# A one-core hybrid encoder layer: one weight conversion moved ahead of the mixed sums on ScalarE, and 144 transposes of the identity added on TensorE around three phase borders

## The chip, the cores and the metric

The kernel runs on one core of a Trainium2 chip. The metric is the device time in microseconds of one execution; the kernel before takes 3360.77 us (median of 3 runs, 3360.53 to 3361.61). The engines are TensorE (PE, its weight loads PEld), VectorE (DVE), ScalarE (ACT), GpSimd (POOL) and SyncE (SP), which issues most of the transfers. TensorE's clock has two levels, 2.4 and 1.2 GHz; the profile gives the granted clock as a share of the upper one.

## The reference

One layer over 2048 tokens of width 1024, float32:

```python
xn = rms_norm(h, g_attn_pre);  proj = xn @ w_in                       # 1024 -> 2304
ya = mixer_a(qa, ka, va)   # grouped-query attention, q/k normalised and rotated, softmax over all keys
yb = mixer_b(qb, kb, vb)   # three dilated windows with a relative-position bias, merged
y  = concat(rms_norm(ya, g_out_a), rms_norm(yb, g_out_b)) @ w_out
h  = h + rms_norm(y, g_attn_post)
f  = square(relu(rms_norm(h, g_mlp_pre) @ w_ff1)) @ w_ff2             # 1024 -> 4096 -> 1024
h  = h + rms_norm(f, g_mlp_post)
h  = h + sigmoid(rms_norm(h, g_ple) @ w_ple_gate) * (p @ w_ple_proj)
```

## The kernel before, in words

**Phases.** Four phases stand one behind the other, each a block of five engine programs with a barrier of all engines at its end: `project_phase`, `mixer_a_phase`, `mixer_b_phase`, `feed_phase`. Order inside a phase is written out by hand; engines meet only through semaphores, and each engine works its own list strictly in order.

**Numbers.** A float32 product is made of two parts. A matrix x is split into an upper half (x rounded to the matmul type, by a copy) and a lower half (x minus the upper half); three matmuls per pair of tiles (`PAIRS`) then give the product.

**The feed phase** walks over 4 blocks of 512 tokens. For each it does the MLP in 4 groups g. A group has 22 weight chunks, listed in `FF`: eight chunks f0 to f7 (24 matmuls each) make the hidden layer, then fourteen chunks (12 matmuls each) make the second MLP product in seven block products n = 0 to 6 of a fast 2x2 scheme (BLOCK_OF, GOES_TO), with two chunks q = 0, 1 for each. They are called 0.0, 0.1, 1.0, 1.1, 2.0 and so on here. Products 0 and 1 take plain quarters of the hidden layer. Products 2 to 6 take sums of quarters, the **mixed sums**: for each of four row groups m of the hidden layer VectorE forms five sums (`mix`, L2394 to L2398), ScalarE writes their upper half (`mixed_hi`, L2191), VectorE their lower half (`mixed_lo`, L2387). TensorE waits before chunk 2.0 for the lower half of the last row group, m = 3.

**Weight chunks.** A raw chunk lands in one of four slots of `w_raw` and is split into one of four slots of `w_sp` (which bear the names feed_v_hl twice, feed_qT and feed_kT, since they lie in the memory of those). For f chunks GpSimd makes both halves (L1860, L1863). For the others ScalarE makes the upper half (`weight_hi`, L2186) and GpSimd the lower (`low`, L1863). `weight_hi` of chunk i waits for its transfer and for TensorE to have begun chunk i - 3; TensorE waits for the lower half. `weight_hi(i + 3)` stands at step i of ScalarE's list.

**Gathering.** When a block product is done, VectorE adds it to two areas of `total` (`gathered`, L2413, eight instructions of 128x512 for products 0 and 1; L2410 where it is the first of a block). Chunk 2.0 writes the banks of product 0, so its first half (t = 0) waits for VectorE's second add, and its second half for the fourth. These adds stand behind `mixed_lo(g, 3)` in VectorE's list.

**Borders.** TensorE's last work in a phase is L446/L449 (project), `fold_out` in the mixers. In mixer B it then starts with four transposes of the identity (L1469) into score banks and waits for its first keys; in the feed phase with `turn(0, 0)`, eight transposes of the first normalised rows, and `first_out(0, 0)` (L1991).

Of the kernel before, what the change touches and what calls it, by code (L numbers as in the profile page):

```python
# [20 lines left out]
P = 128  # L21
# [15 lines left out]
BANK = 512  # L37
# [153 lines left out]
def project_phase(nc, x, w_in, g_pre, g_q, g_k, rope, ident_d, rel_bias, onehot, scr, step, ident, first):  # L191
# [21 lines left out]
    with ExitStack() as ctx:  # L213
# [168 lines left out]
        def _(pe):  # L382
# [39 lines left out]
            for it in range(NBLK // 2):  # L422
                for u in range(2):
                    b = it * 2 + u
                    for i in range(NCH):
                        c = NCH * u + i
                        if b == 0 and i == 0:
                            bias_product(b, 0)
                            continue
                        g = GROUP_OF[i]  # L430
                        n_k = 8 if g == 1 else 4
                        width = CH // n_k
                        k0 = 4 if i > 0 and GROUP_OF[i - 1] == g else 0
                        first, last = k0 == 0, k0 + n_k == KD
                        pe.wait_ge(w_lo, it * (2 * NCH) + NRAW + c + 1)
                        w = [h[:, c % NSPL, :].rearrange("p (k n) -> p k n", k=n_k) for h in w_sp]
                        for t in range(TT):
                            if i == 0:
                                pe.wait_ge(lo_done, b * (2 * TT) + 2 * t + 2)
                            if first:  # L440
                                pe.wait_ge(evicted, b * (NG * TT) + TT * g + t + 1)
                            for kk in range(n_k):
                                for q, (a, m) in enumerate(PAIRS):
                                    begin, end = first and kk == 0 and q == 0, last and kk == n_k - 1 and q == 2
                                    if g in DIMS_FIRST:
                                        mm = pe.matmul(acc[t][:], w[a][:, kk, t * P:(t + 1) * P], xT[u][m][:, k0 + kk, :],  # L446
                                                       start=begin, stop=end)
                                    else:
                                        mm = pe.matmul(acc[t][:, 0:width], xT[u][a][:, k0 + kk, t * P:(t + 1) * P],  # L449
                                                       w[m][:, kk, :], start=begin, stop=end)  # L450
                            if last:
                                mm.then_inc(acc_done, 1)
                        if not last:
                            mm.then_inc(w_used, 1)
                        if i % 2 == 1 and b + 1 < NBLK:
                            turn(b + 1, i // 2)
                        if i in BIAS_AT:
                            bias_product(b, BIAS_AT[i])

        @block.scalar  # L460
        def _(act):
# [682 lines left out]
def mixer_b_phase(nc, scr, step, ident, heads, feed, consts):  # L1144
# [13 lines left out]
    with ExitStack() as ctx:  # L1158
# [254 lines left out]
        def _(pe):  # L1413
# [53 lines left out]
            for sc in score:  # L1467
                for at in (BANK, 2 * BANK - P):
                    pe.transpose(sc[:, at:at + P], ident[:], ident[:])  # L1469
            pe.wait_ge(set_done, 2)  # L1470
            pe.wait_ge(pre_lo, len(FIRST_ORDER))
            scores(0, 0, 0)
# [4 lines left out]
            for h in range(NHB):  # L1477
                par = h % 2
                for n in range(NU):
# [11 lines left out]
                    values(N, h, par, n)  # L1491
                    fold_out(N + 1, n - 1)
            fold_out(NHB * NU + 1, NU - 1)

        @block.scalar
        def _(act):
# [139 lines left out]
def feed_phase(nc, x, w_ff2, w_tail, pT_d, scr, out, step, ident, feed):  # L1636
# [45 lines left out]
    with ExitStack() as ctx:  # L1682
# [205 lines left out]
        def _(pe):  # L1888
# [89 lines left out]
            def first_out(t, n):  # L1978
# [15 lines left out]
                                mm.then_inc(w_used, 1)  # L1994
                mm.then_inc(acc_done, 1)

            turn(0, 0)
            for t in range(TT):
                for n in range(2):
                    first_out(t, n)  # L2000
                    at = 2 * t + n
                    if at < 3:
                        turn(1 + at, 1 + at)
                    if at in (4, 6):
                        turn(TT + at // 2 - 2, at // 2 - 2)
# [84 lines left out]
        def _(act):  # L2090
# [89 lines left out]
            def body(b, u, end=False):  # L2180
# [24 lines left out]
                    act.activation(plain(0, half, m), part(m, half, half), ACT.Copy).then_inc(c_hi, 1)  # L2205

                for i, c in enumerate(FF):
                    if i + 3 < NFF and FF[i + 3][0] == "m":
                        weight_hi(i + 3)
                    if c[0] == "f":  # L2210
                        hidden_hi(c[1], c[2])
                        if c[2] % 2 == 0 and c[2] > 0:
                            mixed_hi(c[1], c[2] // 2 - 1)
                    elif c[2:] == (0, 0):
                        mixed_hi(c[1], 3)
                    if i in NORM_Y and not end:
                        t = NORM_Y[i]
                        y_norm(norm_at(b) + t, t, (y_dma, b * 144 + 32 * (t + 1)), y_in)
                    if i in TURN_Y and not end:
                        t = TURN_Y[i]  # L2220
                        turned_hi(turn_at(b) + t, t, 0, xT)
                    if i == p_at(end):
                        act.wait_ge(y_dma, b * 144 + (16 if end else 32 * TT + 16))
                        act.wait_ge(acc_done, acc_at(b) + (2 * NP * (GROUPS - 1) + 2))
                        act.activation(flat(0, 0, 1), y_in[:], ACT.Copy).then_inc(p_hi, 1)
# [423 lines left out]
```

## Time and profile before

| | |
|---|---|
| time, median of 3 runs | 3360.77 us (3360.53 to 3361.61) |
| time of the profiled execution | 3360.36 us |
| its span, first to last instruction | 3358.6 us |
| PE busy | 3294.1 us, 98% of the span |
| DVE, ACT, POOL busy | 68%, 55%, 55% |
| PE L1906 on the chain that ended last | 41% |
| mean granted clock | 0.996 |

Busy shares are means over four phases. What a change is worth is read where an engine waits: the profile names for each idle stretch the instruction that ended it. "L1906" is the line that issues nearly all matmuls of the feed phase. Two instructions of one engine overlap a little in the records (an instruction's record starts while the one before drains), so the spacing of starts is the better measure of a rate.

### The profile page before, as it was taken

How to read it: one execution, taken by the hardware profiler on the slowest of the kernel's cores; microseconds unless marked ns; L12 is line 12 of the kernel's file. 1: busy time of each engine (PE TensorE's matmuls, PEld its weight loads, DVE VectorE, ACT ScalarE, POOL GpSimd, SP SyncE). 2: the span in 40 equal slices, each digit the busy share in tenths (PEclk: the TensorE clock that was granted, in tenths of full speed). 3: DMA queues.
4: the chain of work that ended last, by engine and by line, in shares of the span. 5: the costliest groups of instructions: out<-in, count | busy, mean ns of one | idle time of the engine just before them, and what ended most of it. 6: DMA issues, size and time to landing. Idle time of an engine off the chain costs nothing.

```text
span 3358.6 us, 48304 instructions
## 1 busy us (share of the span) xinstructions
PE 3294.1 (98%) x17246; PEld 2767.0 (82%) x17246; DVE 2278.8 (68%) x4080; ACT 1853.5 (55%) x3576; POOL 1851.7 (55%) x1434
## 2 busy tenths in 40 slices
PE   8999999999999989998999999999999999999999
PEld 7888878888888879997888888888888888888887
DVE  6556579999999989997646565555746556565555
ACT  3221178888888879998434354344543435443333
POOL 5555534454452168883477732777407776057771
PEclk9999999999999999999999999999999999999999
DMA  5554433444442234344244456444474444744444
GB/s 192 165 185 152 142 104 139 154 169 157 157 143 75 62 88 104 95 99 173 78 138 151 151 194 251 144 154 147 163 250 163 147 155 144 262 155 143 143 149 158
DMA packets 223915, 503.39 MB, mean 150 GB/s; under 512 B 105428, under 2 KB 123420, under 8 KB 204476
## 3 DMA queue, kind: packets, MB, share of 16 engines
q1 hardware_dynamic: 214332, 486.57, 43.9%
q10 hardware_dynamic: 9344, 13.73, 1.1%
q8 instruction: 138, 2.26, 0.3%
q14 instruction: 101, 0.83, 0.1%
HBM read 417.09 MB, written 95.58 MB: 153 GB/s over the span
## 4 chain that ended last, share of the span: by engine, by line
PE 44%; DVE 4%; ACT 2%; POOL 2%; issue 1%; DMA 1%; SPq 0%; ACTq 0%; DVEq 0%
PE feed_bank L1906 41%; DVE feed_sums L2397 1%; PE feed_bank L1991 1%; PE feed_bank L1897 1%; POOL feed_v_hl L1863 1%; POOL feed_qT L1863 0%; PE feed_bank L2014 0%; DMA feed_y_in<-scr_yB 0%; DVE feed_xT L2321 0%; ACT feed_rl L2201 0%; ACT feed_rl L2203 0%; PE feed_bank L2046 0%; POOL feed_kT L1863 0%; ACT feed_v_hl L2186 0%; DVE feed_sums L2394 0%
## 5 line engine op out<-in xcount | busy, mean ns | idle before, releaser
L1863 POOL TENSOR_TENSOR feed_v_hl<-feed_w_raw,feed_v_hl 128x1024 fp32r<-128x1024 f32 x176 | 437.6, 2496 | 138.6 <-ACT feed_v_hl L2186 133.0
L1906 PE MATMUL feed_bank<-feed_v_hl,feed_comb 128*128 128x512 f32 x1776 | 416.5, 390 | 3.1 <-POOL feed_v_hl L1863 3.1
L1906 PEld LDWEIGHTS feed_bank<-feed_v_hl,feed_comb 128*128 128x128 f32 x1776 | 331.8, 188 | 74.5 <-POOL feed_v_hl L1863 6.3
L1126 DVE TENSOR_TENSOR mixa_pT<-mixa_turned,mixa_pT 128x512 fp32r<-128x512 f32 x512 | 350.9, 685 | 58.9 <-ACT mixa_pT L1068 52.5
L1068 ACT ACTIVATE mixa_pT<-mixa_turned 128x512 fp32r<-128x512 f32 x512 | 306.7, 599 | 118.7 <-PE mixa_turned L1004 99.6
L949 PE MATMUL mixa_out_acc<-mixa_pT,mixa_v_hl 128*128 128x512 f32 x1028 | 365.7, 437 | 0.2
L2413 DVE TENSOR_TENSOR feed_total<-feed_total,feed_bank 128x512 f32<-128x512 f32 x352 | 223.9, 682 | 190.2 <-PE feed_bank L1906 187.4
L2382 DVE TENSOR_TENSOR feed_comb<-feed_rl,feed_comb 128x256 fp32r<-128x256 f32 x128 | 138.9, 1085 | 312.1 <-ACT feed_comb L2205 311.7
L1906 PE MATMUL feed_bank<-feed_xT,feed_v_hl 128*128 128x512 f32 x1488 | 344.3, 390 | 3.1 <-ACT feed_rl L2201 3.1
L2201 ACT ACTIVATE feed_rl<-feed_bank 128x512 f32<-128x512 f32 x128 | 76.4, 597 | 490.2 <-PE feed_bank L1906 483.5
L1906 PEld LDWEIGHTS feed_bank<-feed_xT,feed_v_hl 128*128 128x128 f32 x1488 | 280.2, 188 | 62.0 <-issue 3.7
L1093 DVE TENSOR_REDUCE mixa_nmax<-mixa_score 128x1 f32<-128x1024 f32 x256 | 312.6, 1221 | 8.1 <-PE mixa_score L936 1.3
L1004 PE MATMUL mixa_turned<-layer_ident,mixa_prob 128*128 128x128 f32 x2048 | 307.2, 273 | 0.9 <-DVE mixa_pT L1126 0.7
L1004 PEld LDWEIGHTS mixa_turned<-layer_ident,mixa_prob 128*128 128x128 f32 x2048 | 251.7, 141 | 59.8 <-DVE mixa_pT L1126 3.7
L1038 ACT ACTIVATE mixa_prob<-mixa_score,mixa_nmax 128x1024 f32<-128x1024 f32 x256 | 286.2, 1118 | 3.7 <-DVE mixa_nmax L1093 3.6
L936 PE MATMUL mixa_score<-mixa_kT,mixa_qT 128*128 128x512 f32 x1024 | 279.5, 394 | 3.6 <-ACT mixa_prob L1038 2.4
L1863 POOL TENSOR_TENSOR feed_qT<-feed_w_raw,feed_qT 128x1024 fp32r<-128x1024 f32 x88 | 221.6, 2518 | 95.8 <-ACT feed_qT L2186 93.1
L1863 POOL TENSOR_TENSOR feed_kT<-feed_w_raw,feed_kT 128x1024 fp32r<-128x1024 f32 x88 | 218.1, 2478 | 38.0 <-ACT feed_kT L2186 35.2
L936 PEld LDWEIGHTS mixa_score<-mixa_kT,mixa_qT 128*128 128x128 f32 x1024 | 191.6, 188 | 50.3 <-ACT mixa_prob L1038 4.2
L1906 PE MATMUL feed_bank<-feed_qT,feed_comb 128*128 128x512 f32 x888 | 213.7, 391 | 2.2 <-POOL feed_qT L1863 2.2
L1906 PE MATMUL feed_bank<-feed_kT,feed_comb 128*128 128x512 f32 x888 | 212.7, 390 | 2.2 <-POOL feed_kT L1863 1.2
L1906 PEld LDWEIGHTS feed_bank<-feed_qT,feed_comb 128*128 128x128 f32 x888 | 165.7, 188 | 39.0 <-POOL feed_qT L1863 4.7
(263 smaller groups left out, 7099.6 us busy)
## 6 DMA issues: line engine op xcount, KB each, us to landing
feed_w_raw<-scr_wT SPq DMA_DIRECT2D x160, 512.0 KB, 3.3
feed_w_raw<-w_tail_dram SPq DMA_DIRECT2D x128, 512.0 KB, 3.5
proj_w_raw<-w_in_dram SPq DMA_DIRECT2D x36, 1024.0 KB, 5.3
feed_v_hl<-scr_wG SPq DMA_DIRECT2D x34, 1024.0 KB, 5.1
feed_w_raw<-w_ff_dram SPq DMA_DIRECT2D x64, 512.0 KB, 3.4
feed_qT<-scr_wG SPq DMA_DIRECT2D x17, 1024.0 KB, 4.8
feed_kT<-scr_wG SPq DMA_DIRECT2D x17, 1024.0 KB, 5.1
scr_table<-scr_bias SPq DMA_DIRECT2D x8, 1520.0 KB, 9.0
```

The source lines that it names most:

```text
L936: mm = pe.matmul(score[:, at * BANK:(at + 1) * BANK], qT[g][:, h, :], kT[g][part][:, kc * BANK:(kc + 1) * BANK], start=part == 0, stop=par ...
L949: mm = pe.matmul(out_acc[half][:], v_hl[:, s, g, :], pT[part][:, s % NR, :], start=s % (NT // 2) == 0 and part == 0, stop=s % (NT // 2) == ...
L1004: mm = pe.transpose(turned[s % 2][:, h * P:(h + 1) * P], prob[w][:, h, s * P:(s + 1) * P], ident[:])
L1038: act.activation(prob[par][:, h, half * 2 * BANK:(half + 1) * 2 * BANK], score[:, 2 * (c % 2) * BANK:2 * (c % 2 + 1) * BANK], ACT.Exp, bia ...
L1068: act.activation(pT[0][:, s % NR, :], turned[s % 2][:], ACT.Copy).then_inc(hi_done, 1)
L1093: ve.tensor_reduce(nmax[:, par, c // G, c % G:c % G + 1], score[:, 2 * (c % 2) * BANK: 2 * (c % 2 + 1) * BANK], AXX, ALU.max, negate=True) ...
L1126: ve.tensor_tensor(pT[1][:, s % NR, :], turned[s % 2][:], pT[0][:, s % NR, :].bitcast(F32), ALU.subtract).then_inc(lo_done, 1)
L1863: pool.tensor_tensor(w_sp[slot][:, 1, :], w_raw[:, slot, :], w_sp[slot][:, 0, :].bitcast(F32), ALU.subtract).then_inc(w_lo, 1)
L1906: mm = pe.matmul(dst, lhs, rhs, start=start, stop=stop)
L2201: act.activation(hidden(m, half), first_bank(b, g, j)[:], ACT.Relu).then_inc(f_relu, 1)
L2382: ve.tensor_tensor(plain(1, half, m), part(m, half, half), plain(0, half, m).bitcast(F32), ALU.subtract).then_inc(c_lo, 1)
L2413: ve.tensor_tensor(at, at, acc[2 * (n % 2) + t][:], ALU.add if sign > 0 else ALU.subtract).then_inc(ev_dve, 1)
```

## The change

In the feed phase, at the step of chunk 0.0 of every group, ScalarE now makes the upper half of chunk 2.0 (`weight_hi(i + 4)`) ahead of the upper half of the last mixed sums; it made it right behind them before, at the step of chunk 0.1, where it is left out now. On TensorE transposes of the identity are added, which nobody reads and which wait for nothing: 24 at the end of the project phase, 36 after the four that mixer B begins with, 28 at the end of mixer B, and in the feed phase 32 ahead of `turn(0, 0)` and 24 behind it.

```diff
--- before.py
+++ after.py
@@ -456,6 +456,8 @@
                         if i in BIAS_AT:
                             bias_product(b, BIAS_AT[i])
+            for _ in range(24):
+                pe.transpose(tp[0][:, 0:P], ident[:], ident[:])
@@ -1467,6 +1469,8 @@
             for sc in score:
                 for at in (BANK, 2 * BANK - P):
                     pe.transpose(sc[:, at:at + P], ident[:], ident[:])
+            for _ in range(36):
+                pe.transpose(score[1][:, BANK:BANK + P], ident[:], ident[:])
@@ -1491,5 +1495,7 @@
             fold_out(NHB * NU + 1, NU - 1)
+            for _ in range(28):
+                pe.transpose(score[0][:, 0:P], ident[:], ident[:])
@@ -1994,7 +2000,14 @@
+            def keep_on(count):
+
+                for _ in range(count):
+                    pe.transpose(acc[3][:, 0:P], ident[:], ident[:])
+
+            keep_on(32)
             turn(0, 0)
+            keep_on(24)
             for t in range(TT):
@@ -2205,13 +2218,14 @@
                 for i, c in enumerate(FF):
-                    if i + 3 < NFF and FF[i + 3][0] == "m":
+                    if i + 3 < NFF and FF[i + 3][0] == "m" and FF[i - 1][2:] != (0, 0):
                         weight_hi(i + 3)
                     if c[0] == "f":
                         hidden_hi(c[1], c[2])
                         if c[2] % 2 == 0 and c[2] > 0:
                             mixed_hi(c[1], c[2] // 2 - 1)
                     elif c[2:] == (0, 0):
+                        weight_hi(i + 4)
                         mixed_hi(c[1], 3)
```

ScalarE's list in the feed phase, block 0, group 1, from the end of f7 on, before. L2201, L2203 and L2205 are the ReLU, the square and the upper half of the plain quarter; L2186 is an upper half of a weight chunk, named by its slot:

```order
 L2201 ACTIVATE feed_rl<-feed_bank 128x512
 L2203 ACTIVATE feed_rl<-feed_rl 128x512
 L2205 ACTIVATE feed_comb<-feed_rl 128x256
 L2186 ACTIVATE feed_v_hl<-feed_w_raw 128x1024
 L2191 ACTIVATE feed_comb<-feed_sums 128x5x256
 L2186 ACTIVATE feed_qT<-feed_w_raw 128x1024
 L2186 ACTIVATE feed_kT<-feed_w_raw 128x1024
```

and the same place after (the lines are numbered 13 higher):

```order
 L2214 ACTIVATE feed_rl<-feed_bank 128x512
 L2216 ACTIVATE feed_rl<-feed_rl 128x512
 L2218 ACTIVATE feed_comb<-feed_rl 128x256
 L2199 ACTIVATE feed_v_hl<-feed_w_raw 128x1024
 L2199 ACTIVATE feed_qT<-feed_w_raw 128x1024
 L2204 ACTIVATE feed_comb<-feed_sums 128x5x256
 L2199 ACTIVATE feed_kT<-feed_w_raw 128x1024
```

The conversion into feed_qT (chunk 2.0) and the mixed sums have changed places; nothing else on ScalarE has moved, and no other engine's list has in the feed phase's blocks. On TensorE this stands at the border of mixer B and the feed phase, before:

```order
 L1465 MATMUL mixb_out_acc<-layer_ident,mixb_o_sum 128x128 x2
 L1158 UNCONDITIONAL_BRANCH
 L1887 UNCONDITIONAL_BRANCH
 L1897 MATMUL feed_bank<-layer_ident,feed_xn 128x128 x8
 L1991 MATMUL feed_bank<-feed_v_hl,feed_xT 128x512 x12
```

and after:

```order
 L1467 MATMUL mixb_out_acc<-layer_ident,mixb_o_sum 128x128 x2
 L1499 MATMUL mixb_score<-layer_ident 128x128 x28
 L1160 UNCONDITIONAL_BRANCH
 L1893 UNCONDITIONAL_BRANCH
 L2006 MATMUL feed_bank<-layer_ident 128x128 x32
 L1903 MATMUL feed_bank<-layer_ident,feed_xn 128x128 x8
 L2006 MATMUL feed_bank<-layer_ident 128x128 x24
 L1997 MATMUL feed_bank<-feed_v_hl,feed_xT 128x512 x12
```

Three runs of transposes are new there (L1499, L2006 twice), and the order of the rest is as it was.

## Rows read from the trace of the kernel before

**Rows 1.** Who TensorE waited for, whole span: us in total, times, longest.

```profile
PE feed_bank L1906 <- POOL feed_v_hl L1863: 3.1, 8, 0.6
PE feed_bank L1906 <- POOL feed_qT L1863: 2.2, 6, 0.4
PE feed_bank L1906 <- POOL feed_kT L1863: 1.2, 2, 0.6
```

**Rows 2.** Timeline, block 0, group 1: start, length, instruction, [idle before].

```profile
1774.32 1.04 ACT L2186 ACTIVATE feed_v_hl<-feed_w_raw 128x1024 fp32r<-128x1024 f32 x1
...
1775.22 2.88 PE L1906 MATMUL feed_bank<-feed_kT,feed_comb 128*128 128x512 f32 x12
1775.44 2.69 POOL L1863 TENSOR_TENSOR feed_v_hl<-feed_w_raw,feed_v_hl 128x1024 fp32r<-128x1024 f32 x1 [1.52 <-ACT feed_v_hl L2186]
...
1775.79 2.62 DVE L2397 TENSOR_TENSOR feed_sums<-feed_rl 128x256 f32<-128x256 f32 x1
...
1778.33 0.41 DVE L2398 TENSOR_TENSOR feed_sums<-feed_rl 128x256 f32<-128x256 f32 x1
1778.78 1.28 ACT L2191 ACTIVATE feed_comb<-feed_sums 128x1280 fp32r<-128x1280 f32 x1 [3.42 <-DVE feed_sums L2398]
1779.96 1.05 ACT L2186 ACTIVATE feed_qT<-feed_w_raw 128x1024 fp32r<-128x1024 f32 x1
1780.09 1.49 DVE L2387 TENSOR_TENSOR feed_comb<-feed_sums,feed_comb 128x1280 fp32r<-128x1280 f32 x1 [1.34 <-ACT feed_comb L2191]
...
1781.09 2.77 POOL L1863 TENSOR_TENSOR feed_qT<-feed_w_raw,feed_qT 128x1024 fp32r<-128x1024 f32 x1 [2.96 <-ACT feed_qT L2186]
1781.49 4.87 DVE L2413 TENSOR_TENSOR feed_total<-feed_total,feed_bank 128x512 f32<-128x512 f32 x8
...
1783.91 3.01 PE L1906 MATMUL feed_bank<-feed_qT,feed_comb 128*128 128x512 f32 x12 [0.37 <-POOL feed_qT L1863]
```

**Rows 3.** Timeline, block 0, group 0: GpSimd and VectorE's sums.

```profile
1666.25 1.23 POOL L1860 TENSOR_SCALAR feed_kT<-feed_w_raw 128x1024 fp32r<-128x1024 f32 x1
1666.49 1.26 DVE L2397 TENSOR_TENSOR feed_sums<-feed_rl 128x256 f32<-128x256 f32 x1
1667.57 2.42 POOL L1863 TENSOR_TENSOR feed_kT<-feed_w_raw,feed_kT 128x1024 fp32r<-128x1024 f32 x1
1667.67 2.59 DVE L2398 TENSOR_TENSOR feed_sums<-feed_rl 128x256 f32<-128x256 f32 x1
```

**Rows 4.** Timeline, block 0, group 3, at chunk 1.0.

```profile
1941.78 1.32 ACT L2191 ACTIVATE feed_comb<-feed_sums 128x1280 fp32r<-128x1280 f32 x1
1942.02 2.42 POOL L1863 TENSOR_TENSOR feed_v_hl<-feed_w_raw,feed_v_hl 128x1024 fp32r<-128x1024 f32 x1 [3.60 <-ACT feed_v_hl L2186]
...
1943.14 2.65 DVE L2387 TENSOR_TENSOR feed_comb<-feed_sums,feed_comb 128x1280 fp32r<-128x1280 f32 x1
...
1944.39 3.66 POOL L1863 TENSOR_TENSOR feed_qT<-feed_w_raw,feed_qT 128x1024 fp32r<-128x1024 f32 x1
```

**Rows 5.** Windows, PE: stretch, length, busy (x), clock, DMA share, GB/s.

```profile
431.83:435.32 3.49, 0.01 (x2) 1.00 0.20 75
1194.62:1204.86 10.24, 6.16 (x17) 0.50 0.48 112
1576.91:1590.54 13.63, 5.08 (x15) 0.50 0.80 316
```

**Rows 6.** Timeline at the start of mixer B.

```profile
1193.88 0.63 PE L1469 MATMUL mixb_score<-layer_ident 128*128 128x128 f32 x4 [1.05 <-PEq L664]
...
1198.70 0.66 PE L1425 MATMUL mixb_score<-feed_kT,feed_qT 128*128 128x384 f32 x1 [4.20 <-DVE mixb_kT L1562]
...
1209.32 0.44 PE L1425 MATMUL mixb_score<-feed_kT,feed_qT 128*128 128x384 f32 x1 [0.89 <-POOL feed_qT L1326]
```

**Rows 7.** The chain that ended last, start of the feed phase: start, length, what.

```profile
1579.07 1.33 ACT feed_junk L2125 x4
...
1582.89 1.13 PE feed_bank L1897 x4
...
1587.43 7.19 PE feed_bank L1991 x24
1594.62 0.87 PE feed_bank L1897 x8
1595.49 5.47 PE feed_bank L1991 x24
```

## The prediction, made before the changed kernel ran

> **What bounds the kernel now.** I read the busy shares first: TensorE is busy 98% of the span, so a change gains only where it fills a gap of TensorE or raises its clock, and it loses wherever it makes TensorE wait. Next the table of who TensorE waited for. In the feed phase it waits 16 times for GpSimd's lower half of a weight chunk (8 + 6 + 2 times), 3.1 + 2.2 + 1.2 = 6.5 us [rows 1]. Looked at group by group, 13 of these waits are alike, 0.37 us each, at chunk 2.0 (all groups but the last one of blocks 0, 1 and 2), and three of 0.6 us lie at a later chunk of those last groups. Then the timeline around one of the 13 [rows 2]. The reader is to see the chain: VectorE's fourth sum L2397 takes 2.62 us where the fifth, L2398, takes 0.41; the fifth ends at 1778.74; ScalarE's mixed upper half follows at 1778.78, the weight's upper half at 1779.96, GpSimd's lower half at 1781.09, and TensorE starts chunk 2.0 at 1783.91 after 0.37 us. Last the clock in windows: it is 0.50, the 1.2 GHz level, for 10.24 us around the start of mixer B and for 13.63 us around the start of the feed phase, and 1.00 through the 3.49 us gap between the project phase and mixer A [rows 5].
>
> **The moved conversion.** It adds and removes nothing; 16 conversions come earlier. It stands ready to run once TensorE has begun chunk 0.1, at 1775.22, and ScalarE has ended the conversion before, at 1775.36; its transfer was ordered when the lower half of chunk 0.0 was done, several us earlier. So it ends near 1776.7, some 3.3 us earlier than the 1779.96 + 1.05 of before, and delays the mixed upper half by nothing, since ScalarE sat idle for 3.42 us ahead of that [rows 2]. On GpSimd the lower half of chunk 2.0 may then follow right behind that of chunk 1.1, at 1778.1 instead of 1781.09, and be done near 1780.7, well before TensorE is free at 1783.54. Taken alone this closes the gap: 13 x 0.37 = 4.8 us.
>
> But what is late next? VectorE's sums read two operands from SBUF, and so does GpSimd's lower half, and the rows show that one runs only when the other doesn't: L2397 is issued at 1775.79, while GpSimd works from 1775.44 to 1778.13, and ends 0.28 us behind it [rows 2]. In the kernel before GpSimd is then idle for 2.96 us, and L2398 passes in 0.41 us. After the change GpSimd has its next instruction waiting at that moment. What then happens, rows 3 show: GpSimd goes from L1860 (ends 1667.48) into L1863; L2397, held since 1666.49, passes in between and ends at 1667.75; and L2398, which comes behind it, is held through all of L1863, 2.59 us. One VectorE instruction per GpSimd instruction. So the fifth sum, the one that ScalarE waits for, takes 2.59 us instead of 0.41: 2.18 us more.
>
> From there: mixed upper half at 1778.78 + 2.18 = 1780.96; its lower half L2387 at 1780.09 + 2.18 = 1782.27, nothing in its way (the lower half of chunk 2.1 can come at 1783.3 only), ended at 1783.76. Behind it in VectorE's list stand the adds L2413, at a spacing of 4.87 / 8 = 0.61 us and 0.68 us for one: the second ended at 1781.49 + 0.61 + 0.68 = 1782.78 before, and ends at 1784.96 now. Chunk 2.0 writes the banks that these adds read and waits for the second, 0.04 us more from release to start: TensorE starts it at 1785.0 instead of 1783.91, **1.1 us later** in place of the 0.37 us gained. The second half of the chunk needs the fourth add, at 1786.2, and comes to it at 1785.0 + 6 x 0.2275 = 1786.4 (5.47 us for 24 matmuls is 0.228 each, [rows 7]). Later adds and weight chunks have 2 us of room. Nothing gives the time back, as TensorE has no other idle in these groups. 13 x 1.1 = **+14.3 us**.
>
> The Trainium skill, page "SBUF — State Buffer", section "SBUF: two separate sides", says that a VectorE instruction with two SBUF inputs and a GpSimd instruction that reads SBUF share an exclusive port pair, that whichever starts first has it for the whole instruction and that the other is blocked. By that rule the conversion brought forward brings GpSimd's claim forward too, in front of the fifth sum, which can't start before the fourth has ended; the sum by it is the same +14.3 us.
>
> Where GpSimd's own span is laid behind the fourth sum (2.69 us, [rows 2]) instead of the hold seen on VectorE, L2398 ends 0.45 us later still and the term is 13 x 1.55 = 20 us; the other end is a hold that costs nothing, -4.8 us. I take the row of the fifth sum itself [rows 3], the same instruction in the same place of its list.
>
> The Trainium skill, page "Perfetto Trace Analysis", section "GPSIMD Engine Instruction", holds GpSimd's recorded spans unreliable and asks for other measures; by it the 20 us would be dropped, which is the choice made above from the VectorE row.
>
> In the last groups of blocks 0, 1 and 2 ScalarE has transposed rows to copy ahead of these steps and the five sums are over by then. There the mixed upper half itself comes one conversion later, 1941.78 + 0.94 = 1942.7, so L2387 asks at 1944.0, still ahead of GpSimd's next instruction at 1944.39, and passes at the same moment as before, when GpSimd is done at 1944.44 [rows 4]. I cost these three at nothing; the room is 0.4 us, and without it L2387 is a GpSimd instruction later, 2.4 us, of which TensorE would feel little.
>
> **The transposes.** One takes 0.87 / 8 = 0.109 us at 2.4 GHz [rows 7].
>
> Project phase to mixer A: 24 x 0.109 = 2.6 us in a gap of 3.49 us, in which TensorE waits for the last stores, at a clock that is 1.00 anyway [rows 5]. Nothing gained; hidden, with 0.9 us of room.
>
> Start of mixer B: 4 + 36 transposes from 1193.88 are over at 1198.24, before TensorE is wanted at 1198.70 [rows 6]. The clock fell at 1194.62, after 1.9 us in which TensorE had hardly worked. If it holds now, the 6.16 us of busy time at half clock [rows 5] would halve: 3.1 us at most. But TensorE waits for GpSimd's query halves at 1209.32 again [rows 6], which a faster clock moves little. Between 0 and 3.1 I take 1.0, nearer to the row with the wait. If the clock falls all the same, the transposes last 1.3 us too long, most of which the same wait swallows.
>
> Start of the feed phase: 28 transposes, 3.1 us, follow mixer B's last work, while its last store is waited for; 32 from 1579.07 to 1582.6, over before `turn(0, 0)` at 1582.89; 24 behind it until 1586.4, over before the first product at 1587.4. With the clock kept, the first 24 matmuls take 5.47 instead of 7.19 us, 1.72 less, and the first four transposes, 1.13 us on the chain, give some 0.35 more [rows 7]: -2.1 us. The bounds are 0, if the clock is low regardless, and 5.08 / 2 = 2.5 [rows 5].
>
> **Sum**, against the profiled execution, 3360.36 us (span 3358.6 and 1.76 around it; 0.4 under the median of the runs, 3360.77): +14.3 - 1.0 - 2.1 = +11.2, so **3371.6 us**, slower by 0.33%.
>
> **Rivals.**
> - *The fifth sum slips in ahead of GpSimd.* Then the gap closes and the whole is 3360.4 - 4.8 - 3.1 = 3352.5 us, faster by 0.24%. For it: in rows 4 a VectorE instruction that had asked before the next GpSimd one passed at once. Against it: there it had asked first; the fifth sum can't, and in rows 3 it did not.
> - *The hold is real, but TensorE waits for the mixed lower half alone* and the adds are no bound: chunk 2.0 starts at 1783.8, 0.1 earlier than before: -1.3 - 3.1, 3356.0 us, within the noise. For it: no row of before shows TensorE waiting for L2413. Against it: there the adds ended 0.8 us before TensorE was free, so they could not be seen, and now they come 2.18 us later.
> - *The clock is low at the borders regardless*, and then 32 transposes last 7.0 us instead of 3.5, `turn(0, 0)` is 3.2 us late and the 24 behind it delay the first product again, some 5 us in all, with 1.3 at mixer B: 3360.4 + 14.3 + 6.3 = 3381.0 us. Against it: a gap of 3.49 us without any work did not lower it [rows 5].
>
> **Chances and range.** Forecast 0.65 (own range 3367 to 3378, from 3.1 us at mixer B to the 20 us term); first rival 0.18; second 0.11; third 0.06. The range 3352 to 3378 leaves out the third and the outer half of the first. A measurement of this kernel tells 0.2% (6.7 us) from no change. Slower by more: nearly all of the forecast and the third rival, 0.68; within: the second, a part of the first and the lower edge of the forecast, 0.18; faster: the rest of the first, 0.14.
>
> **What would show it.** Right: in 13 groups the last sum of m = 3 lasts 2.6 us instead of 0.41, GpSimd's lower halves of chunks 1.1 and 2.0 stand back to back, and TensorE waits some 1.4 us before chunk 2.0, for VectorE's L2413 or its new line, not for GpSimd. The granted clock is 1.00 from 1576 to 1591. Wrong: TensorE's wait at chunk 2.0 is gone or below 0.4 us, or the last sum still takes 0.41 us; or the clock still falls at the start of the feed phase.

## The result and the profile after

| | before | after |
|---|---|---|
| median of 8 runs each | 3360.78 us (3359.0 to 3362.16) | **3371.98 us** (3370.47 to 3373.29) |
| ratio after / before, 95% interval | | 1.0031, 1.0022 to 1.0041 |
| profiled execution | 3360.36 us | 3371.09 us |
| its span | 3358.6 us | 3369.3 us |
| PE busy | 3294.1 us | 3305.2 us |
| mean granted clock | 0.996 | 0.999 |

The change makes the kernel 11.2 us slower; 3371.6 was forecast. First the table of who TensorE waited for, after (us in total, times, longest). It answers [rows 1]:

```profile
PE feed_bank L1912 <- DVE feed_total L2427: 14.2, 9, 1.6
...
PE feed_bank L1912 <- DVE feed_total L2424: 6.3, 4, 1.6
...
PE feed_bank L1912 <- POOL feed_kT L1869: 1.2, 2, 0.6
...
PE feed_bank L1912 <- POOL feed_v_hl L1869: 0.6, 1, 0.6
```

The 13 short waits for GpSimd are gone, and 9 + 4 = 13 waits for VectorE's adds (L2427, and L2424 in the first group of a block) have come, 1.58 us each and 20.5 us together. The three waits of 0.6 us in the last groups of blocks 0 to 2 are as they were. Next the timeline of block 0, group 1, after, answering [rows 2]:

```profile
1772.47 2.88 PE L1912 MATMUL feed_bank<-feed_kT,feed_comb 128*128 128x512 f32 x12
1772.69 2.69 POOL L1869 TENSOR_TENSOR feed_v_hl<-feed_w_raw,feed_v_hl 128x1024 fp32r<-128x1024 f32 x1 [1.52 <-ACT feed_v_hl L2199]
...
1772.96 1.06 ACT L2199 ACTIVATE feed_qT<-feed_w_raw 128x1024 fp32r<-128x1024 f32 x1 [0.34 <-PE feed_bank L1912]
1773.05 2.62 DVE L2411 TENSOR_TENSOR feed_sums<-feed_rl 128x256 f32<-128x256 f32 x1
...
1775.35 2.58 POOL L1869 TENSOR_TENSOR feed_qT<-feed_w_raw,feed_qT 128x1024 fp32r<-128x1024 f32 x1
1775.59 2.61 DVE L2412 TENSOR_TENSOR feed_sums<-feed_rl 128x256 f32<-128x256 f32 x1
1778.23 1.27 ACT L2204 ACTIVATE feed_comb<-feed_sums 128x1280 fp32r<-128x1280 f32 x1 [4.21 <-DVE feed_sums L2412]
...
1779.54 1.49 DVE L2401 TENSOR_TENSOR feed_comb<-feed_sums,feed_comb 128x1280 fp32r<-128x1280 f32 x1 [1.34 <-ACT feed_comb L2204]
...
1780.95 4.86 DVE L2427 TENSOR_TENSOR feed_total<-feed_total,feed_bank 128x512 f32<-128x512 f32 x8
1782.38 3.01 PE L1912 MATMUL feed_bank<-feed_qT,feed_comb 128*128 128x512 f32 x12 [1.58 <-DVE feed_total L2427]
```

The reader is to see one step after the other. ScalarE's conversion into feed_qT (chunk 2.0) stands at 1772.96, 5.3 us ahead of the mixed upper half. GpSimd's lower half of chunk 2.0 follows that of chunk 1.1 without a gap, at 1775.35. VectorE's fifth sum L2412 lasts 2.61 us, where L2398 took 0.41. The mixed upper half waits for it, then the mixed lower half, then the adds, then TensorE. From the start of chunk 0.1 to the start of chunk 2.0 it is now 1782.38 - 1772.47 = 9.91 us; before, 1783.91 - 1775.22 = 8.69 us: 1.22 us more.

Last the clock in the three windows of [rows 5], and the start of the feed phase:

```profile
431.83:435.32 3.49, 2.71 (x25) 1.00 0.20 75
1194.62:1204.86 10.24, 9.18 (x59) 0.89 0.47 112
1576.91:1590.54 13.63, 12.57 (x93) 1.00 0.84 331
```

```profile
1574.87 3.22 PE L1499 MATMUL mixb_score<-layer_ident 128*128 128x128 f32 x28
1578.57 3.68 PE L2006 MATMUL feed_bank<-layer_ident 128*128 128x128 f32 x32 [0.48 <-PEq L1160]
1582.37 1.09 PE L1903 MATMUL feed_bank<-layer_ident,feed_xn 128*128 128x128 f32 x8
1583.30 2.78 PE L2006 MATMUL feed_bank<-layer_ident 128*128 128x128 f32 x24
1586.54 3.02 PE L1997 MATMUL feed_bank<-feed_v_hl,feed_xT 128*128 128x512 f32 x12 [0.46 <-DVE feed_xT L2335]
```

The clock stays at its upper level through the start of the feed phase, and the first 24 matmuls take 5.74 us on the chain instead of 7.19 [rows 7]. Around the start of mixer B it was low from 1193.6 to 1197.0, so the 4 + 36 transposes end at 1199.9 and not at 1198.2.

**Where the 10.7 us between the two spans are**, from the starts of the same instruction in both traces:

| stretch | before | after | difference |
|---|---|---|---|
| up to the start of mixer A | 435.32 | 435.39 | +0.07 |
| mixer A | 758.56 | 758.49 | -0.07 |
| mixer B, first transpose to the product (L1465, now L1467) at 1220.28 | 26.40 | 26.40 | 0.00 |
| from there to mixer B's last product | 354.94 | 354.42 | -0.52 |
| from there to the second f chunk of the feed phase | 96.98 | 95.16 | -1.82 |
| that chunk and the two behind it | 18.01 | 16.44 | -1.57 |
| 13 groups, chunk 2.0 | | | 13 x 1.196 = +15.55 |
| the phase's last part | | | -0.9 |

The -1.57 is no effect of the change: after a wait of 3.1 us for ScalarE at 1669 to 1672 TensorE's clock fell for some 3 us in the profiled execution of before and not in that of after, and it fell there in ten of the twelve kernels below, with and without transposes.

Nor is the -0.52 an effect of the transposes at mixer B's start, since TensorE is at the same place at 1220.28 in both. It arises at one place, where GpSimd's copies wait for a transfer and the sum that TensorE needs (mixb_o_sum) stands behind them on GpSimd. First before, then after:

```profile
1238.29 0.95 POOL L1292 COPY mixb_t_oth<-mixb_t_near 128x384 f32<-128x384 f32 x2 [1.53 <-DMA mixb_t_own<-scr_table]
...
1240.67 0.33 PE L1465 MATMUL mixb_out_acc<-layer_ident,mixb_o_sum 128*128 128x128 f32 x1 [0.38 <-POOL mixb_o_sum L1370]
```

```profile
1237.54 0.95 POOL L1294 COPY mixb_t_oth<-mixb_t_near 128x384 f32<-128x384 f32 x2 [0.75 <-DMA mixb_t_own<-scr_table]
...
1240.14 0.27 PE L1467 MATMUL mixb_out_acc<-layer_ident,mixb_o_sum 128*128 128x128 f32 x1
```

The transfer landed 0.75 us earlier and the wait of 0.38 us was gone. In the kernels below this stretch lasts 354.4 to 355.7 us, with no order by the transposes. The +0.07 of the first line is chance too: the start of mixer A lies between 433.4 and 437.3 in the fourteen traces.

### The profile page after: what moved, and what is told of

The parts are those of the page before. It is cut to its first block, busy times and chain, and to the rows that moved or that the text cites. A ratio compares the mean times of both kernels' runs of the same rounds, so it can differ in the third digit from the quotient of the medians.

```text
span 3369.3 us, 48592 instructions
## 1 busy us (share of the span) xinstructions
PE 3305.2 (98%) x17390; PEld 2780.3 (83%) x17390; DVE 2305.0 (68%) x4080; ACT 1854.9 (55%) x3576; POOL 1852.3 (55%) x1434
## 4 chain that ended last, share of the span: by engine, by line
PE 43%; DVE 5%; ACT 3%; issue 1%; DMA 1%; POOL 0%; SPq 0%; DVEq 0%; ACTq 0%
PE feed_bank L1912 41%; DVE feed_sums L2412 1%; DVE feed_sums L2411 1%; PE feed_bank L1997 1%; PE feed_bank L1903 1%; ACT feed_comb L2204 1%; DVE feed_total L2427 1%; PE feed_bank L2027 0%; ACT feed_xT L2147 0%; PE feed_bank L2059 0%; DMA feed_y_in<-scr_yB 0%; ACT feed_rl L2214 0%; ACT feed_rl L2216 0%; POOL feed_kT L1869 0%; DVE feed_sums L2408 0%
## 5 line engine op out<-in xcount | busy, mean ns | idle before, releaser
L2396 DVE TENSOR_TENSOR feed_comb<-feed_rl,feed_comb 128x256 fp32r<-128x256 f32 x128 | 148.2, 1158 | 308.4 <-ACT feed_comb L2218 308.0
L2427 DVE TENSOR_TENSOR feed_total<-feed_total,feed_bank 128x512 f32<-128x512 f32 x352 | 224.3, 682 | 180.5 <-PE feed_bank L1912 177.6
```

What stands on the lines that cost most here:

```text
L2396: ve.tensor_tensor(plain(1, half, m), part(m, half, half), plain(0, half, m).bitcast(F32), ALU.subtract).then_inc(c_lo, 1)
L2427: ve.tensor_tensor(at, at, acc[2 * (n % 2) + t][:], ALU.add if sign > 0 else ALU.subtract).then_inc(ev_dve, 1)
```

## The experiments

Each of the twelve was timed in five rounds beside the kernel before on the same chip, and every ratio is against that. The twelve ran in four batches, each on another chip. "Moved" is the conversion ahead of the mixed sums, "transposes" the 144.

### Moved alone

All five loops of transposes are left out of the changed kernel:

```diff
-            for _ in range(28):
-                pe.transpose(score[0][:, 0:P], ident[:], ident[:])
...
-            keep_on(32)
             turn(0, 0)
-            keep_on(24)
```

Expected: 

> The conversion moved, no transposes. Port theory (GpSimd's lower half of chunk 2.0, ready too early, holds VectorE's last sum): the whole loss is here, 13 groups x 1.2 us later at chunk 2.0 less 0.9 us at the end, as in the changed kernel's trace: about 3360.8 + 14.7 = 3375.5 us. Rival (the transposes cost something, the moved conversion less): under 3372 us.

Measured: 3375.16 us (3373.56 to 3376.03), ratio 1.0043, 1.003 to 1.0055. The table of waits of this kernel:

```profile
PE feed_bank L1906 <- DVE feed_total L2419: 14.3, 9, 1.6
...
PE feed_bank L1906 <- DVE feed_total L2416: 6.4, 4, 1.6
```

The same 13 waits of 1.6 us. The whole loss, and more than the whole of the change, is in the moved conversion.

### Transposes alone

```diff
-                    if i + 3 < NFF and FF[i + 3][0] == "m" and FF[i - 1][2:] != (0, 0):
+                    if i + 3 < NFF and FF[i + 3][0] == "m":
...
-                        weight_hi(i + 4)
```

Expected: 

> The transposes, the conversion where it was before. Port theory: a gain of 2 to 4 us, 3357 to 3359 us; 13 waits of 0.37 us at chunk 2.0 as before; granted clock 1.00 at the start of the feed phase and still low for a while at the start of mixer B. Rival (transposes cost): over 3361 us.

Measured: 3356.4 us (3353.93 to 3362.23), ratio 0.9991, 0.9982 to 1.0, with the 8 + 6 + 2 waits for GpSimd of [rows 1] unchanged. -4.2 us against its own kernel before (3360.57 us), at the edge of what can be told: the interval ends at 1.0, and two of the eleven executions took 3361.5 and 3362.2 us.

### Changed kernel, GpSimd held at chunk 2.0

```diff
                             pool.wait_ge(w_hi_ff, it * (4 * NP * GROUPS) + (u * 2 * NP * GROUPS + ff))
+                            if FF[i][2:] == (2, 0):
+                                pool.wait_ge(s_step, step_at(2 * it + u, FF[i][1], 3))
```

GpSimd now waits for the fifth sum (s_step) ahead of this one lower half. ScalarE's order stays as changed.

Expected: 

> The changed kernel, but GpSimd waits with the lower half of chunk 2.0 until VectorE's last sum of m = 3 is done. Port theory: the last sum is back at 0.41 us, GpSimd starts chunk 2.0 about 6.3 us behind the start of chunk 0.0 and is done 2.2 us before TensorE wants it: no wait at chunk 2.0, 13 x (1.58 - 0) = 20.5 us faster than the changed kernel, less about 1 us at the end: 3352 to 3354 us. Rival (the order on ScalarE is what costs: the mixed upper half behind one more conversion): as the changed kernel, 3372 us.

Measured: 3356.99 us (3354.49 to 3361.19), ratio 0.9992, 0.9983 to 1.0. 15 us are back, so it is GpSimd's early start and not ScalarE's order that costs. But TensorE still waits. Its timeline, block 0, group 1:

```profile
1778.73 0.41 DVE L2414 TENSOR_TENSOR feed_sums<-feed_rl 128x256 f32<-128x256 f32 x1
1779.18 1.27 ACT L2206 ACTIVATE feed_comb<-feed_sums 128x1280 fp32r<-128x1280 f32 x1 [2.02 <-DVE feed_sums L2414]
1779.30 2.41 POOL L1869 TENSOR_TENSOR feed_qT<-feed_w_raw,feed_qT 128x1024 fp32r<-128x1024 f32 x1 [0.77 <-DVE feed_sums L2414]
...
1780.49 2.56 DVE L2403 TENSOR_TENSOR feed_comb<-feed_sums,feed_comb 128x1280 fp32r<-128x1280 f32 x1 [1.34 <-ACT feed_comb L2206]
...
1782.97 3.66 DVE L2429 TENSOR_TENSOR feed_total<-feed_total,feed_bank 128x512 f32<-128x512 f32 x6
1784.39 1.83 PE L1914 MATMUL feed_bank<-feed_qT,feed_comb 128*128 128x512 f32 x7 [0.46 <-DVE feed_total L2429]
```

The fifth sum is back at 0.41 us, and the hold has moved on: the mixed lower half L2403 asks at 1780.49, while GpSimd works from 1779.30 to 1781.71, and takes 2.56 us where it took 1.49. My expectation of no wait missed this; a hold of 1.1 us at another instruction leaves 13 waits of 0.46 us.

### Changed kernel, two adds ahead of the mixed lower half

```diff
                         if c[2:] == (0, 0):
+                            gathered(c[1], 0, (0,))
                             mixed_lo(c[1], 3)
                         if c[3] == 1:
-                            gathered(c[1], c[2])
+                            gathered(c[1], c[2], (0, 1) if c[2] else (1,))
```

The adds of the first half (t = 0) of product 0 come first; `gathered` takes only the named halves.

Expected: 

> The changed kernel, but VectorE makes the two adds that chunk 2.0 waits for ahead of the lower half of the mixed sums, in the 1.3 us in which it waits for ScalarE. The last sum is still held (2.6 us). If the adds behind the lower half are what TensorE waits for, as predicted: TensorE waits for the lower half alone, 0.4 instead of 1.58 us, 13 x 1.2 = 15 us faster than the changed kernel, 3357 us. If the mixed lower half is the bound: no change, 3372 us.

Measured: 3356.18 us (3354.08 to 3358.92), ratio 0.9987, 0.9979 to 0.9996.

```profile
1775.34 2.61 DVE L2412 TENSOR_TENSOR feed_sums<-feed_rl 128x256 f32<-128x256 f32 x1
1777.87 1.27 DVE L2427 TENSOR_TENSOR feed_total<-feed_total,feed_bank 128x512 f32<-128x512 f32 x2
...
1779.29 1.49 DVE L2401 TENSOR_TENSOR feed_comb<-feed_sums,feed_comb 128x1280 fp32r<-128x1280 f32 x1 [0.15 <-ACT feed_comb L2204]
...
1780.89 3.00 PE L1912 MATMUL feed_bank<-feed_qT,feed_comb 128*128 128x512 f32 x12 [0.34 <-issue]
```

The fifth sum is held for 2.61 us as in the changed kernel, and still TensorE's wait falls from 1.58 to 0.34 us, behind the mixed lower half. So the last link of the chain was the adds that stand behind it, as forecast, and the second rival (only the mixed lower half bounds) is refuted.

### The hold at chunk 1.1, three times

The edit is that of chunk 2.0 with `(1, 1)` in place of `(2, 0)`, made in the changed kernel, in the kernel before, and in the one with transposes alone.

Expected, in the changed kernel: 

> The changed kernel, with GpSimd's lower half of chunk 1.1 held until the fifth sum of m = 3 is over (in place of chunk 2.0). Theory (GpSimd's lower halves and VectorE's two-operand sums exclude each other, and the order in which they ask decides): the fourth and fifth sum take 0.42 us each, the mixed upper half starts some 4.3 us earlier, the mixed lower half asks while chunk 1.1 is being worked and passes between it and chunk 2.0, before GpSimd's next instruction; TensorE's wait at chunk 2.0 (0.37 us before, 1.58 after the change) is gone in 13 groups: 3372.0 - 20 = 3352 us. Rival (the hold only moves on, as with the wait at chunk 2.0): the mixed lower half is held through chunk 2.0's lower half too, 2.5 us; then the second add is over at the same moment as TensorE gets free and 0.3 to 0.5 us of wait stay: 3357 us.

Expected, in the kernel before: 

> The kernel before, its order of ScalarE kept and no transposes, with the same wait ahead of the lower half of chunk 1.1. Theory: what made TensorE wait 0.37 us for chunk 2.0 in the kernel before was the fourth sum's 2.2 us of hold, and not the conversion's place in ScalarE's list; with the hold gone the 13 waits are gone without moving anything: 3360.6 - 4.8 = 3355.8 us, and TensorE waits for GpSimd in the three last groups only (1.7 us). Rival (ScalarE's order is what makes chunk 2.0 late): the waits of 0.37 us stay, 3360.6 us.

Expected, with transposes and the conversion in its old place: 

> The transposes, the conversion in its old place, and the wait ahead of the lower half of chunk 1.1. Theory: the two gains add, 4.2 us for the transposes as measured and 4.8 for the waits at chunk 2.0: 3351.6 us; and the same as with the conversion moved, within 1 us, since the moved conversion has 2 us of room at either place. Rival: moving the conversion is worth something of its own once the sums are free; then this one is slower than the one with the conversion moved by 13 x 0.37 = 4.8 us.

| | median | ratio, 95% |
|---|---|---|
| changed kernel + hold | **3347.3 us** (3347.12 to 3349.34) | 0.9961, 0.9948 to 0.9973 |
| kernel before + hold | 3352.28 us (3350.1 to 3355.46) | 0.9974, 0.9963 to 0.9985 |
| transposes + hold | 3348.29 us (3346.85 to 3350.64) | 0.9964, 0.9951 to 0.9976 |

All three beat both kernels. The timeline of the first, block 0, group 1:

```profile
1771.42 2.88 PE L1914 MATMUL feed_bank<-feed_kT,feed_comb 128*128 128x512 f32 x12
...
1772.00 0.42 DVE L2413 TENSOR_TENSOR feed_sums<-feed_rl 128x256 f32<-128x256 f32 x1
1772.33 0.42 DVE L2414 TENSOR_TENSOR feed_sums<-feed_rl 128x256 f32<-128x256 f32 x1
1772.88 1.26 ACT L2206 ACTIVATE feed_comb<-feed_sums 128x1280 fp32r<-128x1280 f32 x1
1772.90 2.40 POOL L1869 TENSOR_TENSOR feed_v_hl<-feed_w_raw,feed_v_hl 128x1024 fp32r<-128x1024 f32 x1 [2.78 <-DVE feed_sums L2414]
...
1774.17 2.48 DVE L2403 TENSOR_TENSOR feed_comb<-feed_sums,feed_comb 128x1280 fp32r<-128x1280 f32 x1 [1.42 <-ACT feed_comb L2206]
...
1775.26 3.66 POOL L1869 TENSOR_TENSOR feed_qT<-feed_w_raw,feed_qT 128x1024 fp32r<-128x1024 f32 x1
1776.58 4.86 DVE L2429 TENSOR_TENSOR feed_total<-feed_total,feed_bank 128x512 f32<-128x512 f32 x8
...
1779.59 2.66 PE L1914 MATMUL feed_bank<-feed_qT,feed_comb 128*128 128x512 f32 x11
```

Fourth and fifth sum take 0.42 us each. GpSimd starts chunk 1.1 right behind them. The mixed lower half is held behind it (2.48 us) and passes before GpSimd's chunk 2.0, which is held in its turn (3.66 us); both are still over before TensorE gets there, and chunk 2.0 follows chunk 1.1 without a wait. Chunk 0.1 to chunk 2.0 is 1779.59 - 1771.42 = 8.17 us, 3 x 2.72, TensorE's own rate.

The expectations came out 3.3 to 4.7 us too high, in the main for the same reason each time: I had priced the wait of the kernel before at the 0.37 us of idle time in the record. By the spacing of starts it costs more, in two parts. Chunk 2.0 starts 8.69 - 8.17 = 0.52 us late. And behind a wait its 12 matmuls take longer, 3.01 us in the record where they take 2.88 without one, so that chunk 2.1 starts 2.85 us behind it and not 2.72. First before, then the kernel with the hold:

```profile
1783.91 3.01 PE L1906 MATMUL feed_bank<-feed_qT,feed_comb 128*128 128x512 f32 x12 [0.37 <-POOL feed_qT L1863]
1786.76 2.88 PE L1906 MATMUL feed_bank<-feed_kT,feed_comb 128*128 128x512 f32 x12
```

```profile
1779.59 2.88 PE L1914 MATMUL feed_bank<-feed_qT,feed_comb 128*128 128x512 f32 x12
1782.31 2.88 PE L1914 MATMUL feed_bank<-feed_kT,feed_comb 128*128 128x512 f32 x12
```

That is 0.52 + 0.13 = 0.65 us a group and 13 x 0.65 = 8.5 us, against 3360.52 - 3352.28 = 8.2 measured in the kernel before. The timeline and the kernel before with the hold show what made chunk 2.0 late in the kernel before too: the fourth sum, held 2.2 us by GpSimd's chunk 1.1, and nothing in ScalarE's order. With the sums free, moving the conversion is worth 3348.29 - 3347.3 = 1.0 us, less than either range is wide.

### Which transposes pay

Four kernels have the conversion in its old place and only some of the transposes; a fifth adds the hold at chunk 1.1 to the second of them. Each edit takes out the other loops, as in the first experiment.

Expected, only 32 + 24 in the feed phase: 

> The kernel before with only the 32 + 24 transposes around the first turned rows of the feed phase; none at the end of the project phase, at the start or the end of mixer B. Theory (only the transposes that stand in the feed phase's own start pay, those at mixer B's start buy nothing since TensorE waits for GpSimd's query halves at 1209.3 anyway): TensorE's first products of the feed phase run at the upper clock, 2.3 us gained, 3358.3 us. Rival (the clock has fallen by the time the feed phase begins, since the end of mixer B has gaps with no work in it): the 32 transposes run at half clock, 7.0 us instead of 3.5, and the first product starts later: up to 3 us lost, 3363.5 us.

Expected, 28 at mixer B's end and 32 + 24: 

> The kernel before with the 28 transposes at the end of mixer B and the 32 + 24 of the feed phase, none at the end of the project phase and none at the start of mixer B. Without the 28 the 32 ran at half clock (6.21 us) and nothing was gained. Theory (the three runs at this border work only together, and they are all that pays of the 144): 3356.4 us as with all of them, to 3357.5. Rival (the 36 at mixer B's start carry part of the 4.2 us): 3358.3 us or more.

Expected, only 36 at mixer B's start: 

> The kernel before with only the 36 transposes at the start of mixer B. Theory (TensorE waits there for GpSimd's query halves at 1209.3 in any case): no change, 3360.6 us. Rival (the clock kept there brings the later work forward): up to 3.1 us, half of the 6.16 us of low-clock work of rows 5: 3357.5 us. Where the clock falls all the same in the profiled run, the transposes end late and the wait swallows it.

Expected, 28 + 32 + 24 and the hold: 

> The conversion in its old place, the wait ahead of the lower half of chunk 1.1, and only the 28 + 32 + 24 transposes of mixer B's end and the feed phase's start. Theory (each of the two mechanisms stands for itself): 3360.6 - 8.2 (the wait alone) - 4.2 (the transposes) = 3348.2 us, as with all 144. Rival (the 36 at mixer B's start are needed): 3350 us or more.

Expected, only 24 at the end of the project phase: 

> The kernel before with only the 24 transposes at the end of the project phase. In the profiled execution of the kernel before the clock is 1.00 at the start of mixer A, and mixer A lasts 758.56 us to the start of mixer B; in the six other profiled kernels without these transposes it fell there, and mixer A lasts 759.3 to 759.9; in the six with them it is 1.00 and 758.5. Theory (the profiled execution of before was a lucky one, and the 24 transposes hold the clock at this border): clock 1.00 from 432 to 440, mixer A 758.5 us, and the time 0.8 to 1.3 us under the median of before: 3359.7 us, which the timing alone can't tell from none. Rival (chance, as with the stretch at 1670): the clock may be low here too and mixer A last 759.3 or more; 3360.8 us.

| kernel | median | ratio, 95% |
|---|---|---|
| only 32 + 24 | 3360.9 us | 0.9999, 0.999 to 1.0008 |
| 28 and 32 + 24 | 3359.77 us | 0.9995, 0.9986 to 1.0004 |
| only 36 | 3359.82 us | 0.9997, 0.9988 to 1.0005 |
| only 24 | 3360.51 us | 1.0, 0.9991 to 1.0009 |
| 28 + 32 + 24 and the hold | 3350.73 us (3348.14 to 3357.16) | 0.9971, 0.9961 to 0.9981 |

No time of the first four is told from no change. The profiled execution of the fifth, 3356.78 us, is one of two of its nine that took 3357 us; the other seven took 3348.1 to 3352.2. The traces tell more. The feed phase's start with only 32 + 24:

```profile
1579.00 6.21 PE L2000 MATMUL feed_bank<-layer_ident 128*128 128x128 f32 x32 [3.54 <-PEq L1158]
1585.05 1.04 PE L1897 MATMUL feed_bank<-layer_ident,feed_xn 128*128 128x128 f32 x8
1585.92 2.78 PE L2000 MATMUL feed_bank<-layer_ident 128*128 128x128 f32 x24
1589.07 3.01 PE L1991 MATMUL feed_bank<-feed_v_hl,feed_xT 128*128 128x512 f32 x12 [0.37 <-DVE feed_xT L2328]
```

Without the 28 that fill the 3.54 us in front, the clock falls in that gap, the 32 take 6.21 us instead of 3.68, `turn(0, 0)` comes 2.2 us later than in [rows 7], and most of the gain is gone. This is the third rival's mechanism, real but absent from the changed kernel's profiled execution. It can come with all 144 too: in the kernels with the hold at chunk 2.0 and with two adds first the clock fell among the 28, and `turn(0, 0)` came 1.5 us later.

The lengths of three stretches over all fourteen profiled kernels (us; starts of the same instructions):

| stretch | without its transposes | with them |
|---|---|---|
| mixer A (24 at the end of the project phase) | 758.56 once, 759.3 to 759.9 six times | 758.4 to 758.5, seven times |
| start of mixer B, first transpose to the product of 1220.28 (36) | 26.4, seven times | 25.6 where the clock was kept at the border (four), 26.3 to 26.4 where it fell (three) |
| mixer B's end to the second f chunk (28, 32, 24) | 97.0 to 98.2 (five); 97.3 with only 32 + 24 | 95.2 where the clock was kept (five), 96.7 where it fell among the 28 (three) |

The one 758.56 is the profiled execution of the kernel before. Its clock from 432 to 440 is in the first line, that of the kernel with only the 36 in the second, that of the one with only the 24 in the third (us, PE busy (x), clock, DMA share, GB/s):

```profile
432.00:440.00 8.00, 3.52 (x27) 1.00 0.49 163
```

```profile
432.00:440.00 8.00, 4.77 (x26) 0.79 0.58 183
```

```profile
432.00:440.00 8.00, 5.97 (x43) 1.00 0.67 205
```

So the 24 do hold the clock at that border, and are worth about 1 us in most executions, none in the one that the forecast was made from. Over the typical execution the 144 bring, by the means of each cell, 1.0 at mixer A (759.5 over the seven without against 758.5), 0.5 at mixer B's start (26.4 against 25.9) and 2.1 at the feed phase's start (97.8 against 95.7), 3.6 us in all, which fits the 4.2 measured. That is a sum of readings of single executions; the timing of the parts, whose intervals are some 6 us wide, neither confirms nor denies it. The kernel with the hold and without the 24 and 36 is 2.4 us above the one with all 144, again within what the two intervals leave open.

## Why the prediction was right, step by step

- **The moved conversion.** Forecast: it ends near 1776.7 in the times of before, GpSimd's chunk 2.0 follows chunk 1.1 at once, and the fifth sum takes 2.59 us. All three are in the timeline after: the conversion ends 1.55 us behind the start of chunk 0.1, as forecast, and the sum takes 2.61 us. (The forecast calls that 3.3 us earlier; 1781.01 - 1776.7 is 4.3. Nothing in the sum used it.) The kernel with GpSimd held at chunk 2.0 shows it to be the cause: the same order on ScalarE, the fifth sum at 0.41 us, 15 us less. That is also what refutes the first rival, in which the sum slips in first. The row that decided was [rows 3]: of VectorE's instructions one passes between two of GpSimd's that stand back to back, and the next is held.
- **What is late next.** Forecast: the second add, TensorE 1.1 us later, a wait of about 1.4 us for L2413's new line. Measured: 1.58 us of wait and 1.196 us of delay per group. The 0.1 us that was missing lies between the second add's end and TensorE's start: 1780.95 + 0.61 + 0.68 = 1782.24 to 1782.38 is 0.14, and 0.04 was taken. 13 x 0.1 = +1.25 us.
- **The last groups of blocks 0, 1, 2** at nothing: right, their waits are the same three of 0.6 us.
- **Border 1** at nothing: right against this trace, wrong as a statement on the kernel, since [rows 5] showed a clock that was kept once and falls in six of the seven kernels without the 24 transposes.
- **Mixer B's start**, -1.0 within 0 to -3.1: nothing in this execution, where the clock fell all the same from 1193.6 to 1197.0 and later waits swallowed the longer transposes, as the forecast had it for that case. Where the clock was kept it is 26.40 - 25.56 = 0.84 us; there waits for GpSimd and VectorE take the rest (1.3, 0.7, 0.7 and 0.6 us up to 1211 in the changed kernel with the hold at chunk 1.1), and not the one for the query halves alone. The -0.52 of the table is the transfer's.
- **Feed phase's start**, -2.1: -1.8, with clock 1.00 from 1576 to 1591.
- **Not foreseen:** -1.57 us from a low-clock stretch near 1672 that came in one profiled execution and not in the other, and -0.9 us at the end of the phase, where an instruction of VectorE (L2447 before, L2461 after) took 3.29 us before and 2.58 us after, and TensorE's next transposes came 0.7 us sooner. Why it was held for less no experiment shows.

Sum: forecast +11.2, measured +10.7 in the traces and +11.2 in the medians. In the traces the misses are +1.25 (adds), +1.0 (mixer B's start), +0.3 (feed phase's start), -1.57 (clock near 1672), -0.9 (the phase's end) and -0.52 (the transfer): they cancel to -0.5. In the medians of the parts the moved conversion gives +14.6 where +14.3 was forecast, and the transposes -4.2 where it was -3.1. So the large term was right by its mechanism; that the total came out within half a microsecond is luck.

One price in the prediction was too low without bearing on the forecast: closing the gap was put at 13 x 0.37 = 4.8 us, and the kernel before with the hold gained 8.2. The first rival would have been some 3 us faster than it says.

## What to carry to other kernels

Before bringing an instruction forward, look at who shares something with its follower: here an idle gap of 2.96 us on GpSimd looked like slack and was the slot in which VectorE's last sum got through. When a wait names one engine, go back along the chain to the first instruction that lasts longer than its equals (2.62 where its neighbour takes 0.41); holding the other engine back there, with one wait, gave 8.2 us in the kernel before, where moving the named instruction lost 14.6. A clock read from one profiled execution says what happened once: transposes that fill a gap are worth the mean over executions. At the border to the feed phase they paid only where they began at the start of the gap.

## What the runs showed of the hardware

- A hold moves to the next instruction that reads two operands from SBUF. With GpSimd's lower half at 1779.30 to 1781.71 the mixed lower half took 2.56 us instead of 1.49; with it at 1772.90 to 1775.30, 2.48. Where VectorE had asked first, GpSimd's own instruction was recorded at 3.66 instead of 2.40 us. The Trainium skill, page "SBUF — State Buffer", section "SBUF: two separate sides", has the pair of ports go for the whole instruction to whichever starts first; both rows agree. What happens when instructions of both engines are queued, this case shows: they take turns, here and in [rows 3] and [rows 4].
- VectorE's adds with one operand in a TensorE bank keep their spacing of 4.86 / 8 = 0.61 us beside a lower half of GpSimd (1780.95 to 1785.81 after, beside GpSimd from 1780.54 to 1783.27), the same as the 4.87 of [rows 2].
- The first 12 matmuls behind a wait take 3.01 us in the record, those in a row 2.88, and the next chunk starts 0.13 us later for it. So the idle time in the record (0.37 us) is less than what a wait costs (0.65 us by the spacing of starts).
- The same gap lowers the clock in some executions and not in others: 3.5 us without work at the border to mixer A kept 1.00 in one of seven kernels. The Trainium skill, page "TensorE: Matmul & The Clock Gate", section "What's actually happening", says that the number of slow matmuls at a kernel's start varies from run to run; here it does so in the middle of a kernel too, and mixer A was 0.8 to 1.3 us longer in the other six kernels than in that one.
- Transposes don't always keep the clock either: at mixer B's start it fell in three of the seven profiled kernels that have the 36, though only 1.05 us of idle time lay just ahead of the first.
